# Fourth scores directly behind the fourth level, and the rows of ScalarE and VectorE turned to match, in the heads of block 1

## The reference

```python
h = rmsnorm(x, attn_norm[layer])
proj = h @ w_in[layer]
(a_q, a_k, a_v, b_q, b_ff, b_fb, b_i, b_g, gate_a, gate_b) = split_columns(proj)
y_a = diff_attention(a_q, a_k, a_v, cos, sin, da_lambda[layer], da_norm[layer], layer) @ w_a[layer]
y_b = hgrn2_bidirectional(b_q, b_ff, b_fb, b_i, b_g, ...) @ w_b[layer]
merged = jax.nn.sigmoid(gate_a) * y_a + jax.nn.sigmoid(gate_b) * y_b
x = x + merged @ w_o[layer]
h = rmsnorm(x, ffn_norm[layer])
x = x + (jax.nn.silu(h @ w_gate[layer]) * (h @ w_up[layer])) @ w_down[layer]
```

```python
s = jnp.einsum('bqhcd,bkhcd->bhcqk', qi, k).astype(jnp.float32)
p = jax.nn.softmax(s, axis=-1)
w = p[:, :, 0] - lam_full * p[:, :, 1]
return jnp.einsum('bhqk,bkhv->bqhv', w.astype(v.dtype), v)
```

## Time and profile before

| | us |
|---|---|
| median of 3 runs (3588.12 to 3590.41) | 3589.61 |
| the profiled execution | 3584.19 |
| its span | 3582.4 |
| TensorE busy in the span | 3506.2 |
| VectorE busy | 1934.6 |
| ScalarE busy | 1386.9 |
| GpSimd busy | 468.7 |

### The profile page before, as it was taken

One profiled execution on the slowest core, in us unless ns is written; L12 is line 12 of the kernel. 1 busy time (PEld: TensorE's weight loads), 2 busy tenths in 40 slices (PEclk: granted clock), 3 DMA queues, 4 the chain that ended last, 5 costly groups with the idle time before them and its releaser, 6 DMA issues.

```text
span 3582.4 us, 44557 instructions
## 1 busy us (share of the span) xinstructions
PE 3506.2 (98%) x16012; PEld 2810.9 (78%) x16012; DVE 1934.6 (54%) x2485; ACT 1386.9 (39%) x1950; POOL 468.7 (13%) x320
## 2 busy tenths in 40 slices
PE   7999999999999999999999999999999999999998
PEld 5777788888777788888888866788878887678886
DVE  6888544433888654433444487633263327873334
ACT  4455443323445443322333255432243224653223
POOL 2333110001333210001200110200020003020002
PEclk9999999999999999999999999999999999999999
DMA  3111222223111232222322211222222222122222
GB/s 109 65 61 63 100 94 94 100 94 118 65 59 65 73 111 97 96 96 98 106 97 96 94 65 56 88 98 94 99 84 98 94 99 83 54 71 94 100 94 100
DMA packets 87378, 315.42 MB, mean 88 GB/s; under 512 B 9952, under 2 KB 10592, under 8 KB 86880
## 3 DMA queue, kind: packets, MB, share of 16 engines
q1 hardware_dynamic: 84384, 305.48, 25.1%
q10 hardware_dynamic: 2880, 8.39, 0.7%
HBM read 309.64 MB, written 4.19 MB: 88 GB/s over the span
## 4 chain that ended last, share of the span: by engine, by line
PE 89%; DVE 6%; DVEq 2%; ACT 1%; issue 1%; DMA 1%; POOLq 0%; SPq 0%; ACTq 0%; POOL 0%
PE ps L1760 22%; PE ps L1762 21%; PE ps L1761 21%; PE sc L1760 5%; PE sc L1761 5%; PE sc L1762 5%; DVE w_lo L1073 2%; PE ps L1928 2%; DVE h_lo L1520 1%; PE sc L1915 1%; PE ps L1853 1%; PE sc L2001 1%; DVEq L1378 1%; DVEq L1544 1%; DVE stg L1359 1%
## 5 line engine op out<-in xcount | busy, mean ns | idle before, releaser
L1073 DVE TENSOR_TENSOR w_lo<-raw,w_hi 128x1024 fp32r<-128x1024 f32 x574 | 733.8, 1278 | 1117.7 <-ACT w_hi L524 1117.4
L524 ACT ACTIVATE w_hi<-raw 128x1024 fp32r<-128x1024 f32 x574 | 608.8, 1061 | 1442.3 <-PE ps L1762 771.0
L1760 PE MATMUL ps<-h_hi,w_hi 128*128 128x512 f32 x2576 | 1049.8, 408 | 23.3 <-DVE h_lo L1083 23.1
L1762 PE MATMUL ps<-h_hi,w_lo 128*128 128x512 f32 x2576 | 1005.6, 390 | 0.0
L1761 PE MATMUL ps<-h_lo,w_hi 128*128 128x512 f32 x2576 | 1004.8, 390 | 0.0
L1760 PEld LDWEIGHTS ps<-h_hi,w_hi 128*128 128x128 f32 x2576 | 484.5, 188 | 150.7 <-issue 62.9
L1762 PEld LDWEIGHTS ps<-h_hi,w_lo 128*128 128x128 f32 x2576 | 484.0, 188 | 103.9
L1761 PEld LDWEIGHTS ps<-h_lo,w_hi 128*128 128x128 f32 x2576 | 485.2, 188 | 97.0 <-issue 9.1
L1760 PE MATMUL ps<-hid_hi,w_hi 128*128 (+1 forms) x792 | 309.7, 391 | 0.0
L1762 PE MATMUL ps<-hid_hi,w_lo 128*128 (+1 forms) x792 | 308.2, 389 | 0.0
L1761 PE MATMUL ps<-hid_lo,w_hi 128*128 (+1 forms) x792 | 308.2, 389 | 0.0
(11 more groups left out here) (314 smaller groups left out, 4345.7 us busy)
## 6 DMA issues: line engine op xcount, KB each, us to landing
raw<-wts SPq DMA_DIRECT2D x574, 512.0 KB, 3.2
x<-xT SPq DMA_DIRECT2D x1, 2048.0 KB, 10.5
x<-xT ACTq DMA_DIRECT2D x1, 2048.0 KB, 8.8
parked<-x ACTq DMA_DIRECT2D x8, 256.0 KB, 2.0
x<-parked ACTq DMA_DIRECT2D x1, 2048.0 KB, 8.1
outT<-x SPq DMA_DIRECT2D x8, 256.0 KB, 2.1
mask_in<-m ACTq DMA_DIRECT2D x1, 448.0 KB, 12.6
moves<-c ACTq DMA_DIRECT2D x1, 320.0 KB, 3.2
```

Source lines behind the costliest of these rows:

```text
L524: act(w_hi[:, s].rearrange("p a b -> p (a b)"), raw[:, s, :], ACT.Copy).then_inc(s_whi, 1)
L1073: tt(w_lo[:, s].rearrange("p a b -> p (a b)"), raw[:, s, :], w_hi[:, s].rearrange("p a b -> p (a b)").bitcast(F32), ALU.subtract).then_inc ...
L1760: mm(out, w_hi[:, s, b, :], hi, start=start, stop=False, skip_group_check=True)
L1762: return mm(out, w_lo[:, s, b, :], hi, start=False, stop=stop, skip_group_check=True)
```

## The change

TensorE issues the fourth scores directly behind the fourth level; the fill steps are regrouped, so that the number up to the fifth level falls by two and the number behind it rises by two. ScalarE does the fourth block's two exponentials (and the third block's scaling) ahead of `weights_out(1)` and `split_next(2)`. VectorE makes the third block's weights ahead of `take_fill(2)` and `split_next(2)`. No instruction is added or removed.

```diff
@@ ACT, one head
                     exps(5)
                     decays(h, 5)
-                    weights_out(1)
-                    split_next(2)
                     scale_first(2)
                     exps(6)
                     exps(7)
+                    weights_out(1)
+                    split_next(2)
                     decays(h, 6)
@@ DVE, one head
                     level(4)
+                    weights(2)
                     take_fill(2)
                     split_next(2)
-                    weights(2)
                     level(5)
@@ PE, one head
                     level(3)
+                    scores(3)
                     fill(2)
                     turn_weights(1)
-                    fill(1)
-                    scores(3)
-                    fill(3)
+                    fill(2)
                     level(4)
-                    fill(4)
+                    fill(6)
                     turn_weights(2)
```

## The result

| | before | after |
|---|---|---|
| median of five executions, us | 3589.58 | 3565.41 |
| lowest and highest | 3588.12, 3590.41 | 3562.65, 3565.43 |
| ratio of after to before | | 0.9931 (95% interval 0.9917 to 0.9945) |
| the profiled execution | 3584.19 | 3565.41 |
| its span | 3582.4 | 3563.6 |

By the medians the change takes 24.2 us; by the two profiled executions it takes 18.8. The forecast was 20 and 3569.6. Two things have to be explained, and they pull in opposite directions: why the heads gave a little less than forecast, and why the medians gave more.

What follows compares the result with a forecast made beforehand. TensorE and VectorE were taken to wait for each other once per head, in a chain through block 3's scores. Gaining 2.5 us in each of eight heads, 20 us, takes 3589.6 to 3569.6; own range 3565.5 to 3573, with rivals 3565 to 3577.

Steps and rivals of the forecast that it cites:

- What bounds the kernel: In each head block 2's transposes wait 2.5 us for weights(2), in a chain from block 3's scores; 20.3 us in eight times.
- TensorE's order: scores(3) directly behind level(3) meet no new wait; block 2's transposes start at 110.3 instead of 113.10 in the first head.
- VectorE's order: Block 3's row maximum starts at 102.1, what follows moves 2.6 us forward; weights(2) end near 107.5, 2.8 us ahead of TensorE.
- ScalarE's order: exps(6) start at 104.1, the weights' high half is ready at 106.9, decays(6) end at 107.9; TensorE needs weights_out(1) only from 110.3.
- rivals 3 and 4: 3: scores(3) wait until their old place, 3589.6, chance 0.05. 4: scores(3) wait longer, slower, 3600, chance 0.03.
- What is late next: The fifth chunk's first fill step waits 0.3 to 0.4 us for VectorE's split, held by GpSimd's Y(6); 2.5 us gained per head.
- rival 1: No hold: in the first head the split comes before Y(6), which waits; 2.9 us gained per head, 3566.6; chance 0.18.
- rival 2: Level 6's product on VectorE, with the least slack left, becomes TensorE's stall; gain 1.7 us per head, 3576; chance 0.14.
- The sum: 2.5 us per head in eight heads, 20 us: 3564.2 against the profiled execution, 3569.6 against the runs' median, 5.4 above it.
- The range: 3565.5 to 3573, from a split hold of none to 0.6 us and 1.5 run spread; 3565 to 3577 with rivals 1 and 2.

## Why the prediction was right or wrong, point by point

**What bounds the kernel.** Right. One chain through the scores of block 3, of which TensorE's wait and VectorE's gap were the two ends; moving the scores alone brought all of it.

**TensorE's order, VectorE's order, ScalarE's order.** Right to 0.1 or 0.2 us at every station: transposes 110.37 (110.3), row maximum 102.18 (102.1), weights(2) 105.59 (105.5), exps(6) 104.25 (104.1). No wait at scores(3), so rivals 3 and 4 fell.

**What is late next.** Right in its mechanism: a new wait of 0.3 us of L1760 on the split, and the hold by Y(6) shown by cutting Y(6) short. Its size was too small. I forecast that the fifth chunk starts at 10.93 behind level(3)'s start in every head; in six heads it was 11.28, because Y(6) ended 10.14 behind level(3)'s start instead of 9.8, and the split with it. In the other two the split won by 0.01 us, as rival 1 had it, and the hold fell on level 5's product; of the 2.78 won there 0.2 were given back at level(6), a small form of rival 2. Together 18.8 us instead of 20 between the two profiled executions.

**The sum.** This is the step that failed: "the median of the runs is 5.4 above that execution, so 3589.6 - 20". I took the 5.4 us for something that is there with and without the change, and gave no reason for it. They were part of the price of the stalls. Before has ten stalls of 2.5 to 2.6 us, eight in the heads and two behind them, and each may be followed by a stretch at half the clock, which costs about 1.5 us. The profiled execution had two such stretches, both behind the heads, where the change takes nothing away. By the same price a median of 3589.6 means five or six, so with both of those three or four in the heads, and these went with the stalls: 3.6 x 1.5 = 5.4 us. Filling the stall with idle matmuls takes them away, lengthening it brings them in every head. After has only the two stalls behind the heads; its median execution is the profiled one, with both stretches (3565.4), and the medians moved by 24.2. Executions of the first five themselves were not profiled, so their number of stretches is an estimate; the nearest that was seen is an execution of 3588.1 us with three in the heads and two behind them. In the later series before's median of 3583.9 means about two and after's 3562.5 none, and the change brought 21.4 there: on the forecast's 3589.61 that ratio gives 3568.8, inside the range. How near the forecast came thus depends on how many stretches a series happened to have, and so does it that the first result lies near rival 1's 3566.6, although the hold is there in every head, on the split or on level 5's product. Why one stall is followed by the lower clock and the next, equally long, is not, stays open.

**The range.** Its lower end counted 2.9 us per head and the runs' spread of 1.5 (3566.6 less 1.5 is 3565.1, where the text has 3565.5), and nothing for a stall that costs more than it lasts. The spread of before alone, 2.3 us in three executions, did not show it; 27 executions span 9 us.

## What to carry to other kernels

When two engines each wait for the other once per round, find the one operation whose place starts the chain and move that alone; rows turned on other engines "to match" can cost what they were to save. A stall of TensorE can be worth more than its length, since the clock may be lower behind it (seen here behind stalls of 2.1 us and longer, about 1.5 us each time): price it with that. Count the stretches of lower clock in each profile, over the whole span and not only where the change lies, before two executions are compared; when the profiled one is faster than the median, ask whether the stall to be removed is what the others lose. Before two operations of VectorE are turned, look which of them GpSimd can hold.

## What the runs showed of the hardware that I had not expected

- TensorE's granted clock fell to one half behind stalls of 2.5 us in none, two and three of eight heads of three profiles with the same stall, each time for a stretch like 368.1 to 371.5; behind stalls of 2.1 us in four of eight, behind stalls of 4.53 us in eight of eight. Behind the 0.8 us that were left of the filled stall it fell in none of eight, and behind the waits of 1.5 us in none of 28.
- One such stretch cost 1.4 to 1.6 us, and after's executions lie in steps of that size.
- Two fp32 matmuls without use, 1.7 us of work in each stall, did not make the kernel slower, and its median was lower: 3582.6 against 3585.7.
- Where an operation of VectorE and one of GpSimd start within some hundredths of a microsecond, either can be the one that is held: VectorE's split, 0.01 us ahead, ran its 1.21 us and Y(6) took 3.13; VectorE's product, 0.02 us behind, ran its 0.68 and Y(6) took 2.61. With 0.1 us between them the split was held for the whole of Y(6), 2.97 us. It fell the same way in the same heads in both profiles of the changed kernel.
